# Rows of the expert passes: from scatter, reads and transposes to products with a one-hot matrix

## The reference, cut to what matters

```
p_group, group_idx = lax.top_k(group_prob, 1)
top_p, top_i = lax.top_k(jax.nn.softmax(in_group, axis=-1), TOP_K)      # TOP_K = 2
expert_id = (group_idx * EXPERTS_PER_GROUP + top_i).reshape(m)          # m = 1024 pairs
...
x_rows = xf[row_tok].reshape(n_blocks, MOE_BLOCK, d)
hcat = xb @ w13[e]
hid = jax.nn.silu(hcat[:, :EXPERT_FF]) * hcat[:, EXPERT_FF:]            # EXPERT_FF = 512
y = jax.ops.segment_sum((hid @ w2[e]) * row_gate[:, None], row_tok, num_segments=n)
```

## Time and profile before

| | us |
|---|---|
| median of 3 runs | 3893.95 |
| the three runs | 3892.6, 3900.96, 3893.95 |
| the profiled execution's own time | 3898.67 |
| its span, first to last instruction | 3897.1 |
| TensorE busy | 3204.2 (82%) |
| VectorE busy | 1021.3 (26%) |
| ScalarE busy | 730.3 (19%) |
| mean granted TensorE clock | 0.92 of 2.4 GHz |

### The profile page before, as it was taken

How to read it: one execution, slowest core, us unless ns; L and a number is a source line. 1 busy time by engine, 2 the same in 40 slices (tenths; PEclk the granted TensorE clock), 3 DMA queues, 4 the chain that set the end, 5 groups by cost and what they waited for, 6 DMA issues and landing times. The chain is left out here.

```text
span 3897.1 us, 39468 instructions
## 1 busy us (share of the span) xinstructions
PE 3204.2 (82%) x16187; PEld 1635.7 (42%) x16187; DVE 1021.3 (26%) x1990; ACT 730.3 (19%) x1460; POOL 246.9 (6%) x228
## 2 busy tenths in 40 slices
PE   5897998587765899658777559789999889889998
PEld 3443984232221446323222135456644445346443
DVE  1332642200001207330000120266500220266202
ACT  1320242000000004100000020435500010335200
POOL 0002520000000000100000000210000000110000
PEclk9998998799997999879898879899999999989999
DMA  5344111899999431369999722111011101211120
GB/s 191 108 154 202 55 45 52 350 427 418 397 402 371 151 130 44 98 264 428 418 390 400 311 73 58 27 41 44 23 43 43 43 33 43 49 41 44 48 83 22
DMA packets 163906, 639.56 MB, mean 164 GB/s; under 512 B 58164, under 2 KB 60722, under 8 KB 138000
## 3 DMA queue, kind: packets, MB, share of 16 engines
q1 hardware_dynamic: 144784, 557.44, 37.2%
q10 hardware_dynamic: 10368, 50.34, 3.2%
q0 software_dynamic: 8576, 29.26, 2.1%
HBM read 584.44 MB, written 56.48 MB: 164 GB/s over the span
## 5 line engine op out<-in xcount | busy, mean ns | idle before, releaser
L1455 PE MATMUL banks<-weight_ring,experts_xT 128*32 128x512 f32 (+1 forms) x2240 | 394.5, 657 | 100.5 <-DMA weight_ring<-in_moe_w 80.6
L2335 PE MATMUL banks<-weight_ring,cols 128*128 128x512 f32 (+1 forms) x928 | 363.9, 553 | 14.2 <-PEq L2476 8.2
L1473 PE MATMUL banks<-weight_ring,experts_hT 128*32 128x512 f32 (+1 forms) x1216 | 249.6, 648 | 44.0 <-DMA weight_ring<-in_moe_w 44.0
L2335 PEld LDWEIGHTS banks<-weight_ring,cols 128*128 128x128 f32 x928 | 167.5, 192 | 208.0 <-issue 207.8
L1455 PEld LDWEIGHTS banks<-weight_ring,experts_xT 128*32 128x32 f32 (+1 forms) x2240 | 117.9, 127 | 324.3 <-issue 261.8
L2335 PE MATMUL banks<-weight_ring 128*128 128x512 f32 x480 | 207.0, 593 | 4.6 <-PEq L2878 2.7
L1455 PE MATMUL banks<-cols,experts_xT 128*32 128x512 f32 (+1 forms) x640 | 182.0, 636 | 23.8 <-DMA cols<-in_moe_w 18.1
L1473 PE MATMUL banks<-cols,experts_hT 128*32 128x512 f32 (+1 forms) x448 | 171.9, 638 | 21.5 <-DMA cols<-in_moe_w 21.5
L1455 PE MATMUL banks<-experts_slot,experts_xT 128*32 128x512 f32 (+1 forms) x448 | 167.9, 633 | 18.2 <-DMA experts_slot<-in_moe_w 18.2
L2335 PE MATMUL banks<-cols,weight_ring 128*128 128x512 f32 x416 | 179.8, 592 | 1.9 <-PEq L272 1.9
L2581 ACT ACTIVATE pairs_p<-banks,pairs_low 128x768 f32<-128x768 f32 (+1 forms) x160 | 130.3, 815 | 221.0 <-DVE pairs_low L2636 128.6
(11 more groups left out here) (414 smaller groups left out, 4305.9 us busy)
## 6 DMA issues: line engine op xcount, KB each, us to landing
weight_ring<-in_moe_w SPq DMA_DIRECT2D x132, 2048.0 KB, 22.0
cols<-in_moe_w SPq DMA_DIRECT2D x40, 2048.0 KB, 27.8
experts_slot<-in_moe_w SPq DMA_DIRECT2D x20, 2048.0 KB, 28.8
weight_ring<-in_w_in SPq DMA_DIRECT2D x16, 2048.0 KB, 7.8
weight_ring<-in_w_ada SPq DMA_DIRECT2D x12, 2048.0 KB, 11.2
weight_ring<-in_a_w_in SPq DMA_DIRECT2D x8, 2048.0 KB, 10.9
experts_xin<-block_rows_in ACTq DMA_DIRECT2D x32, 512.0 KB, 16.5
block_rows_out<-experts_y ACTq DMA_DIRECT2D x32, 512.0 KB, 10.8
```

The costliest lines, as they stand in the source:

```text
L1455: mm = pe.matmul(bank[a:a + n, :], self.xT[:, 4 * part + k, a:a + n], slots(r, part)[:, k, c:c + 512], start=part == k == 0, stop=part == ...
L1473: mm = pe.matmul(self.out[c][a:a + n, :], self.hT[:, f, a:a + n], slots(r, 2)[:, f, c * 512:c * 512 + 512], start=f == 0, stop=f == 3)
L2335: mm = pe.matmul(ps[i % 8][0:u.shape[0], 0:u.shape[1]], u.lhs(w, k), u.rhs(w, k), start=k == 0, stop=k == u.kd - 1)
```

## The change

The rows of a pass are no longer scattered, read and transposed. For every pass VectorE compares `dest` with 0 to 127 and adds the two comparisons (`select`): `sel` is, for each of four groups of 128 tokens, a 128 x 128 matrix with a one where the token goes to that row of the pass; then it subtracts 128 from `dest` for the next pass. `turn` multiplies `K.H` by `sel` and sums over the four groups in the bank, 32 products of 128 x 128 by 128 in place of eight transposes. The columns come out as before and `take_cols` is unchanged. The scatter, the `xin` loads and six of the eight clearing DMAs go. The scaling of `K.H` by ALPHA moves from ahead of the passes to behind them, `order` comes ahead of `rows` on VectorE, TensorE no longer waits for `order` ahead of `turn(0)`, four small instructions build `iota` at the stage's start, and in the first layer the sum for lambda, with its wait for `K.loaded`, moves from the middle of the routing chain to behind `ei`. Declarations that only follow from this are left out of the diff.

```
 def clear_block_rows(eng, X, zeros):
-    for row in range(0, ROWS, 4 * P):
-        eng.dma_start(X.xs[row:row + 4 * P, :].rearrange("(p b) d -> p (b d)", p=P), zeros).then_inc(X.cleared, 16)
...
-        self.xin = [sb(f"xin{i}", [P, D]) for i in range(2)]
+        self.sel = sb("sel", [P, 2, NT, P])
+        self.sel1 = sb("sel1", [P, NT, P])
+        self.dest = sb("dest", [P, NT, 2])
+        self.iota = sb("iota", [P, P])
...
-    def load_x(self, eng, p):
-        i, _ = self.x_buffer(p)
-        eng.dma_start(self.xin[i][:, :], self.X.xs[bass.ds(p * P, P), :]).then_inc(self.s["x"][i], 16)
+    def select(self, dve, p):
+        if not isinstance(p, int):
+            dve.wait_ge(*self.freed("turned", p, 2))
+        elif p >= 2:
+            dve.wait_ge(*self.passed("turned", p - 2, 2))
+        if not isinstance(p, int) or p:
+            dve.wait_ge(*self.freed("based", p))
+            dve.wait_ge(*self.freed("selected", p))
+        to = self.sel[:, self.sel_buffer(p), :, :]
+        for j, x in enumerate((to, self.sel1[:, :, :])):
+            dve.tensor_tensor(x, bm(self.iota[:, :], NT), bc(self.dest[:, :, j], P), ALU.is_equal).then_inc(self.s["picked"], 1)
+        dve.wait_ge(*self.passed("picked", p, 2))
+        dve.tensor_tensor(to, to, self.sel1[:, :, :], ALU.add).then_inc(self.s["selected"], 1)
+        dve.tensor_scalar(self.dest[:, :, :], self.dest[:, :, :], float(-P), None, ALU.add).then_inc(self.s["based"], 1)
 
     def turn(self, pe, p):
         ps = self.K.ps
-        i, count = self.x_buffer(p)
-        pe.wait_ge(self.s["x"][i], count)
+        pe.wait_ge(*self.passed("selected", p))
         for half in range(2):
             for k in range(4):
-                mm = pe.transpose(ps[half][:, k * P:(k + 1) * P],
-                                  self.xin[i][:, :].rearrange("r (p k) -> r k p", k=KD)[:, 4 * half + k, :], self.K.c("ident"))
+                for t in range(NT):
+                    x = self.K.H[:, t, :].rearrange("r (p k) -> r k p", k=KD)[:, 4 * half + k, :]
+                    mm = pe.matmul(ps[half][:, k * P:(k + 1) * P], x, self.sel[:, self.sel_buffer(p), t, :],
+                                   start=t == 0, stop=t == NT - 1)
             mm.then_inc(self.s["turned"], 1)
...
+                B.turn(pe, 0)
                 pe.wait_ge(*V.at("order"))
-                B.turn(pe, 0)
...
-                act.wait_ge(X.scattered, 16 * 2 * NT * X.layers)
-                B.load_x(act, 0)
-                B.load_x(act, 1)
                 B.take_cols(act, 0)
                 act.wait_ge(*V.at("ei"))
                 for p in range(NP):
-                    if p + 2 < NP:
-                        B.load_x(act, p + 2)
                     B.gated(act, p)
...
-                for t in tt:
-                    for j in range(2):
-                        pool.indirect_dma_start(X.xs, bass.IndirectOffsetOnAxis(ap=X.rows[:, t, j:j + 1].bitcast(U32), axis=0),
-                                                K.H[:, t, :], None).then_inc(X.scattered, 16)
...
+                for q in range(4):
+                    dve.tensor_scalar(B.iota[:, 32 * q:32 * q + 32], K.c("iota32"), float(32 * q), None, ALU.add).then_inc(*V(f"iota{q}"))
...
-                if l == 0:
-                    dve.wait_ge(K.loaded, K.n_loaded)
-                    v = par.rearrange("p (a b) n -> p a b n", b=2)
-                    dve.tensor_tensor(prod, v[:, :, 0, :], v[:, :, 1, :], ALU.mult).then_inc(*V("lam_p"))
...
-                dve.tensor_copy(X.rows[:, :, :], dest[:, :, :]).then_inc(*V("rows"))
                 dve.wait_ge(*E.at("order"))
                 dve.tensor_copy(X.order[:, :], order).then_inc(*V("order"))
+                dve.tensor_copy(X.rows[:, :, :], dest[:, :, :]).then_inc(*V("rows"))
+                at("rows")
+                for p in range(2):
+                    B.select(dve, p)
...
                 if l == 0:
+                    dve.wait_ge(K.loaded, K.n_loaded)
+                    v = par.rearrange("p (a b) n -> p a b n", b=2)
+                    dve.tensor_tensor(prod, v[:, :, 0, :], v[:, :, 1, :], ALU.mult).then_inc(*V("lam_p"))
...
-                dve.wait_ge(X.scattered, 16 * 2 * NT * X.layers)
-                for t in tt:
-                    dve.tensor_scalar(K.H[:, t, :], K.H[:, t, :], ALPHA, None, ALU.mult).then_inc(*V(f"scaled{t}"))
                 for p in range(NP):
                     if p:
                         B.hidden_cols(dve, p - 1)
                     B.hidden(dve, p)
+                    if p + 2 < NP:
+                        B.select(dve, p + 2)
                     if p:
                         B.half_y(dve, p - 1)
...
+                for t in tt:
+                    dve.tensor_scalar(H[:, t, :], H[:, t, :], ALPHA, None, ALU.mult).then_inc(*V(f"scaled{t}"))
```

More of the change, by code:

```diff
@@ L1352 @@
 class Experts:
-    POINTS = ["turned", "cols", "first_half", "up", "silu", "hidden", "hidden_turned", "hidden_cols", "down", "y_act", "y_dve"]
+    POINTS = ["picked", "based", "selected", "turned", "cols", "first_half", "up", "silu", "hidden", "hidden_turned", "hidden_cols", "down", "y_act", "y_dve"]
     def __init__(self, K):
         nc = K.nc
-        self.xs = nc.dram_tensor("block_rows_in", [ROWS, D], F32, kind="Internal").ap()
         self.ys = nc.dram_tensor("block_rows_out", [ROWS, D], F32, kind="Internal").ap()
@@ L1375, in sems @@
         s = {x: nc.alloc_semaphore(f"{name}_{x}") for x in self.POINTS}
-        s["x"] = [nc.alloc_semaphore(f"{name}_x_landed_{i}") for i in range(2)]
         s["y"] = nc.alloc_semaphore(f"{name}_y_stored")
@@ L1544, in stage_experts @@
         more_cmp = sb("over_cmp", [P, NE, 8])
-        dest = sb("dest", [P, NT, 2])
+        dest = B.dest
         eb = sb("eb", [P, EXTRA + 1])
@@ L1550, in stage_experts @@
         if l == 0:
-            par = B.xT[:, 0:2, :].rearrange("p k (a n) -> p (k a) n", a=2)
-            prod = B.xT[:, 2, :].rearrange("p (a n) -> p a n", a=2)
+            par = B.y[:, 512:768].rearrange("p (a n) -> p a n", a=4)
+            prod = B.y[:, 768:896].rearrange("p (a n) -> p a n", a=2)
         tot, key, over, nx, xe, jump, one = (per[:, i, :] for i in range(7))
@@ L1583, in stage_experts @@
                           act=["cols", "ex", "ed"] + ["lam"] * (l == 0) + ["stored", "ln", "rs"],
-                          dve=["pad", "one", "cols", "lg0", "lg1", "el0", "el1"] + [f"gm{t}" for t in tt] + [f"gi{t}" for t in tt] +
+                          dve=["pad", "one"] + [f"iota{q}" for q in range(4)] + ["cols", "lg0", "lg1", "el0", "el1"] + [f"gm{t}" for t in tt] + [f"gi{t}" for t in tt] +
                           ["gf", "mask", "low", "masked", "el3"] + [f"v{t}" for t in tt] + [f"i{t}" for t in tt] +
-                          ["idx", "hot0", "hot1", "both", "exd", "dv", "sm", "rs", "e1", "re", "g0", "g1"] + ["lam_p", "lam_s"] * (l == 0) + [
-                           "zero", "k1", "k2", "k3", "tot", "pos", "key", "col", "above", "place_hot", "rooms", "place_col", "numbers",
+                          ["idx", "hot0", "hot1", "both", "exd", "dv", "sm", "rs", "e1", "re", "g0", "g1", "zero", "k1", "k2", "k3", "tot", "pos", "key", "col", "above", "place_hot", "rooms", "place_col", "numbers",
                            "room", "over", "ocmp", "nx", "xe", "xb", "j0", "j1", "jump",
-                           "W0", "past_cut", "W1", "gecap", "gj", "W", "p0", "p1", "r0", "r1", "rows",
-                           "order", "ecmp", "eb", "clip", "nxt", "ei"] + ["lam_d", "lam"] * (l == 0) + [f"scaled{t}" for t in tt] +
+                           "W0", "past_cut", "W1", "gecap", "gj", "W", "p0", "p1", "r0", "r1", "order", "rows",
+                           "ecmp", "eb", "clip", "nxt", "ei"] + ["lam_p", "lam_s", "lam_d", "lam"] * (l == 0) + [f"scaled{t}" for t in tt] +
                           [f"{x}{t}" for t in tt for x in ("b", "c", "st0", "st1", "mv")] + [f"m{t}" for t in tt] + [f"n{t}" for t in tt])
@@ L1722, in _ @@
                 act.activation(dv[:, :], dv[:, :], ACT.Exp).then_inc(*S("ed"))
+                B.take_cols(act, 0)
+                act.wait_ge(*V.at("ei"))
                 if l == 0:
@@ L1743, in _ @@
                     with act.If(has_rows(j, n)):
-                        B.load_x(act, j)
                         B.take_cols(act, j)
@@ L1934, in _ @@
                     with dve.If(has_rows(j, n)):
+                        B.select(dve, j)
                         B.hidden(dve, j)
```

15 lines of the change are left out of this document (5 added, 10 removed).

## The result

The changed kernel takes 4132.38 us (median of 4 runs, 4131.08 to 4133.91), against 3895.95 us (4 runs, 3892.6 to 3900.96) for the kernel before beside it. The ratio is 1.0606, with a 95% interval of 1.0587 to 1.0624. The forecast was 3868 us with a range up to 3898; rival (b) had given 4003.

A forecast was written before the change was run, and what follows sets the result against it. Expert stages: TensorE paces early passes, then a loop of weight loads and TensorE work. -7.2 - 5.2 - 7.5 + 4.0 - 9.8 = -25.7 us, rounded to -26, on 3898.67; against median 3893.95, 3868 us, range 3838 to 3898.

The forecast's parts named there:

- rival (b): Turn's strided K.H read keeps weight loads from hiding under products: 12.3 us a turn, +135, 4003 us; chance 0.06.
- the price of a turn: Each pass's turn: 64 records at 0.114 us, from L2335's group of the same shape: 7.3 us, adding 6.2.
- 27 counting turns: Turns whose extra time counts: nine in the TensorE-paced part, one or two per pair of passes, 13 to 14 a layer.
- the tail: Each layer's end from pass 13, one turn hidden under loads: 87.2 us either way.
- the passes: Passes 2 to 7, paced by TensorE: 22.3 + 6.2 = 28.5 us each, six make 171.
- the pairs: Passes 8 to 13, a loop of loads and TensorE work: 66.2 us per two passes, against 68.7 and 69.5.
- The start: First layer, from `order` to pass 1's silu: 60.9 us, with a first turn of 11.5.
- lambda: First layer's routing chain: 7.9 us leave it as the wait for parameters moves behind `ei`.
- the heads: Heads stage: fewer DMA issues ahead of ScalarE's first exponential (-5.5), no clearing traffic (1.7 us): -7.2, bounds 0 and -9.
- (c): Passes 8 to 13 don't shorten, another transfer or half-clock spells taking the room: 3885 us; chance 0.11.
- (d): TensorE's lower clock persists in the TensorE-paced passes and the loops, about 10 us a layer: 3888 us; chance 0.10.
- (e): Passes 8 to 13 bound by DMA alone, 61.8 us per two passes: -26 more, 3842 us; chance 0.10.

The follow-up runs named there:

- experiment 3: Kernel before, its eight transposes a pass issued as identity products: 3896.49 us against 3900.39; also its transposes reading neighbouring elements, w13 loads in 4 KB pieces: 3942.85 us.
- step one: Changed kernel, turn reading K.H in blocks of 128 neighbouring elements (features meet other w13 rows): 3882.58 us, ratio 0.9955.
- pairs: Changed kernel, features dealt to partitions in twos: turn reads every second element, w13 loads in 8 KB pieces: 3902.85 us, ratio 1.0009.

## Why the prediction was wrong

**The step that failed is the price of a turn.** "The nearest row is the group of L2335 with the same shape": the shape was the same, the access was not (its weight loads read neighbouring elements and take 192 ns, the turn's 334). 0.240 us a record against 0.114 makes 15.4 us a turn against 7.3. The alternative was named as rival (b) with a chance of 0.06, and with L1439 as the evidence against it; that evidence is void (experiment 3), since a transpose and a product price the same read differently.

**Its size.** Rival (b) took one weight load per record, 12.3 us a turn, and 27 counting turns, for +135 us. Measured: 8.1 us more a turn, and with TensorE as the main pace of the whole stage nearly every one of the 32 counts: after less step one, 249.8 us, is 31 times 8.1. In the first layer the end of `order` to pass 1's silu is 20.2 us over the forecast (turns 0 to 2), passes 1 to 7 49.3 over (six turns), passes 7 to 13 47.7 over (six), the tail 9.6 over. "A us on a turn counts in one or two of each pair" holds only while the weights are not far behind.

**The rule on steps.** The Trainium skill ("SBUF — State Buffer", "Door 1: The DMA port swizzle") gives reads up to a step of four float32 as free. The direction was right where I had trusted a row of another operation: step eight is not free. The boundary is not: step two is nearly free (199 ns a load against 195), step four is not (329), and the measurement decides. The same passage of the Trainium skill also wants at least two accesses to each line of 16 bytes; step two gives two and step four one, so that condition fits what was measured.

**Right, and shown with step one:** the passes (28.6 of 28.5) and the pairs (66.7 of 66.2). The start came out too (59.9 us of 60.9), in part by luck: its first turn was 8.9 us, not 11.5, and the rest 1.6 longer, since a second stretch at the lower clock, behind a wait of 3.0 us for the copy, made a gate-up 8.65 us in place of 7.09.

**Right in sum, by luck in part:** `order` 14.0 us earlier, where 15.1 were forecast (7.9 of lambda and 7.2 of the heads). From the layer norm's first instruction to `order` it is 43.8 us after and 50.6 before, so lambda gave 6.8. From the memset to that instruction it is 12.6 us less. But the memset itself stands 5.4 us later (351.19 against 345.83), and that is drift: in *pairs*, with the same code up to there, it stands at 346.77.

**Right as well:** select, `iota`, scaling and ScalarE's shorter queue cost nothing that shows; TensorE waits 14.6 us in all for `selected`, in the two starts and nowhere else.

**Right in mechanism, off in size:** with step one the second layer takes 524.6 us from `order` to the last y, where the forecast's terms add to 516.2 (pairs 3.2 us longer in all, the tail 4.2 longer than before, where no change was forecast). So the kernel that I had in mind is 0.45% faster, not 0.67%, and nearly all of that lies ahead of the first `order`. Rivals (c), (d) and (e) were not it: the pairs did shorten with step one, the clock stayed at 1.00 in the passes that TensorE paces (780 to 860 us) and was 0.96 in the pairs (1000 to 1200 us), and pairs never came to 61.8 us. Rival (d) also misread its row: a mean granted clock of 0.90 between the levels 0.5 and 1.0 is a fifth of the time at 1.2 GHz, not a tenth, so by its own reasoning it should have been priced at about twice the 10 us a layer.

**Open:** why the load of a product suffers more from the step than the load of a transpose; how much of the heads stage's 6.8 us reaches the end, since the clock's dips move with it; and what lambda's move and the missing clearing transfers would give on their own, without the products. No run has them alone.

## What to carry to other kernels

Price a matmul by a row with the same access as well as the same shape: a step of eight float32 on either operand, or of four on the loaded one, halved TensorE's rate here, and an operation of another kind (a transpose) on the same data hid it. Where a layout forces such a step on something read many times, pay for the sorting once, on an engine that is idle: eight copies a layer on ScalarE, and eight instructions of VectorE in its wait for the gather, replaced a penalty in 16 turns. And work that was free while transfers set the pace (92 us of TensorE, in experiment 3) stops being free at a knee that only the loop's own slack tells; price the far side of it with every instance, not with those that counted before. When a change brings along moves that shorten something else, date the events between them: here nearly all that the step-one kernel gained lay ahead of the stages, where the moves alongside act, and 1.2 us in the stages themselves.

## What the runs showed of the hardware

- TensorE, float32, 128 columns: 0.116 us a record with step one, 0.123 with two, 0.236 with four, 0.240 with eight on the loaded operand, and 0.117 and 0.236 with one and eight on the streamed one. A turn that began at a granted clock of 0.50 (up to 709 us) and went on at 1.00 (from 712) took 8.9 us with step one, against 7.4 at 1.00 throughout; with step eight it was 15.48 both times.
- A transpose with step eight: load 193 ns against 142, no more time in the group. The same data as products: load 334 ns.
- ScalarE copying 1024 elements to a partition, read with step eight: 2.08 us against 1.06. VectorE scaling 1024 elements, written with step eight: 1.10 us against 0.72 in place without a step.
- Loads in pieces of 16, 8 and 4 KB: 415, 410 and 395 GB/s per unit of DMA share; the whole kernel before lost 1.2% to pieces of 4 KB.
